# Wide products: the high-weight and the low-weight matmuls of a half, one phase after the other or tile by tile

## The reference, cut to what matters

```python
def conv_ffn(x, w_up, conv_w, conv_b, w_down):
    h = causal_dwconv(x @ w_up, conv_w, conv_b)
    gate, up = jnp.split(h, 2, axis=-1)
    return (jax.nn.gelu(gate) * up) @ w_down
```

## Time and profile before

| | |
|---|---|
| median of 3 runs | 3481.41 us (3480.82 to 3483.87) |
| span of the profiled execution | 3479.9 us |
| TensorE busy | 3388.8 us (97%) |
| VectorE, ScalarE busy | 2255.3 us (65%), 1729.5 us (50%) |
| DMA | 563.65 MB, mean 162 GB/s |
| mean granted TensorE clock | 0.992 |

### The profile page before, as it was taken

The page is one execution under the profiler, slowest core; times in us unless marked ns, Lnnn a source line. Parts: engine busy times, 40 slices in busy tenths (PEclk is TensorE's granted clock), DMA queues, the critical chain, the costliest instruction groups (busy, mean ns, idle before and its releaser), DMA issues.

```text
span 3479.9 us, 51413 instructions
## 1 busy us (share of the span) xinstructions
PE 3388.8 (97%) x20556; PEld 2996.1 (86%) x20556; DVE 2255.3 (65%) x2857; ACT 1729.5 (50%) x2142; POOL 0.2 (0%) x4
## 2 busy tenths in 40 slices
PE   9999998999999999999989999999999999999998
PEld 7888998888888888888878888888888888888887
DVE  6487676666666456555676666755666668556685
ACT  5473234565656335434366556643453555444553
POOL 0000000000000000000000000000000000000000
PEclk9999999999999999999999999999999999999999
DMA  7351034555554554432535544455454533544342
GB/s 278 147 189 47 2 122 146 193 186 183 185 193 151 193 183 179 176 134 77 195 145 193 187 180 187 160 188 184 174 192 147 194 121 146 194 149 188 126 165 102
DMA packets 45943, 563.65 MB, mean 162 GB/s; under 512 B 4928, under 2 KB 7120, under 8 KB 9168
## 3 DMA queue, kind: packets, MB, share of 16 engines
q1 hardware_dynamic: 45776, 561.27, 43.7%
HBM read 559.13 MB, written 2.12 MB: 161 GB/s over the span
## 4 chain that ended last, share of the span: by engine, by line
PE 88%; DVE 6%; ACT 3%; issue 2%; DMA 1%; SPq 0%; DVEq 0%; ACTq 0%
PE bank L765 38%; PE bank L769 20%; PE bank L860 8%; PE bank L865 4%; PE bank L894 3%; PE bank L878 2%; DVE ring L2250 1%; ACT spl_r L1609 1%; PE bank L789 1%; PE bank L1172 1%; DVE spl_r L2250 1%; DVE scr_r L2250 1%; PE bank L699 1%; PE bank L695 1%; PE bank L693 1%
## 5 line engine op out<-in xcount | busy, mean ns | idle before, releaser
L2250 DVE TENSOR_TENSOR spl_r<-ring,spl_r 128x2048 fp32r<-128x2048 f32 (+2 forms) x425 | 951.6, 2240 | 528.2 <-ACT spl_r L1609 526.4
L765 PE MATMUL bank<-all_r,spl_r 128*128 128x512 f32 x4960 | 1200.5, 394 | 5.4 <-ACT spl_r L1609 5.4
L1609 ACT ACTIVATE spl_r<-ring 128x2048 fp32r<-128x2048 f32 x409 | 781.9, 1912 | 612.9 <-PE bank L769 472.0
L765 PEld LDWEIGHTS bank<-all_r,spl_r 128*128 128x128 f32 x4960 | 915.2, 188 | 194.6 <-issue 7.9
L769 PEld LDWEIGHTS bank<-all_r,spl_r 128*128 128x128 f32 x5008 | 642.4, 191 | 28.9 <-DVE spl_r L2250 5.0
L769 PE MATMUL bank<-all_r,spl_r 128*128 128x256 f32 x5008 | 650.4, 283 | 3.7 <-DVE spl_r L2250 3.7
L860 PE MATMUL bank<-scr_r,dsp_r 128*128 128x512 f32 x1408 | 345.2, 393 | 11.6 <-ACT dsp_r L1609 6.1
L2250 DVE TENSOR_TENSOR dsp_r<-ring,dsp_r 128x1408 fp32r<-128x1408 f32 x128 | 208.0, 1625 | 222.5 <-ACT dsp_r L1609 222.5
L1609 ACT ACTIVATE dsp_r<-ring 128x1408 fp32r<-128x1408 f32 x128 | 176.6, 1380 | 281.2 <-PE bank L865 276.7
L860 PEld LDWEIGHTS bank<-scr_r,dsp_r 128*128 128x128 f32 x1408 | 256.4, 188 | 61.8 <-ACT scr_r L1619 6.8
L765 PE MATMUL bank<-scr_r,spl_r 128*128 128x512 f32 x1168 | 282.5, 394 | 3.4 <-ACT spl_r L1609 3.4
(11 more groups left out here) (403 smaller groups left out, 3002.8 us busy)
## 6 DMA issues: line engine op xcount, KB each, us to landing
ring<-in_up SPq DMA_DIRECT2D x88, 2048.0 KB, 7.9
ring<-in_down SPq DMA_DIRECT2D x64, 1408.0 KB, 6.0
ring<-in_ib SPq DMA_DIRECT2D x34, 2048.0 KB, 8.0
ring<-in_pg SPq DMA_DIRECT2D x16, 2048.0 KB, 8.2
ring<-in_out SPq DMA_DIRECT2D x16, 2048.0 KB, 7.9
ring<-in_in SPq DMA_DIRECT2D x12, 2048.0 KB, 8.1
ring<-in_ec SPq DMA_DIRECT2D x11, 2048.0 KB, 8.5
ring<-in_ea SPq DMA_DIRECT2D x8, 2048.0 KB, 10.9
```

The lines of the kernel that those rows point to most:

```text
L765: mm(b[:, :], WHI[half][:, kk, :], pair(name, kk), start=kk == 0, stop=False, skip_group_check=True)
L1609: A(high[half], w[:, :, half * P:(half + 1) * P], ACT.Copy).then_inc(S["w_hi"], count)
L2250: return V.tensor_tensor(out, a, b, op)
```

## The change

Within a half the two phases become one: for each tile the 512-column matmul with the high weights is followed at once by the 256-column matmul with the low weights. The wait for the low weights (`w_lo`) stands ahead of the first matmul of the half, where it stood between the phases. The same is done in the down product. In a `first` half the order of the matmuls stays as it was; only the form of the loop differs. `both_halves`, `first_piece` and the plain `product` are not touched, and neither are the lists of ScalarE, VectorE and the DMA queue.

```diff
@@ wide_half
                     from_low(0, early)
                     if early < DT:
                         from_high(early, DT)
-                else:
-                    for kk in range(DT):
+                pe.wait_ge(S["w_lo"], at(HALF0[name] + half + 1, k, i, 2))
+                for kk in range(DT):
+                    if not first:
                         mm(b[:, :], WHI[half][:, kk, :], pair(name, kk), start=kk == 0, stop=False,
                            skip_group_check=True)
-                pe.wait_ge(S["w_lo"], at(HALF0[name] + half + 1, k, i, 2))
-                for kk in range(DT):
                     one = mm(main, WLO[half][:, kk, :], rhi[:, kk, :], start=False, stop=kk == DT - 1,
                              skip_group_check=True)
@@ down
                             pe.wait_ge(S["w_hi"], ready)
+                            pe.wait_ge(S["w_lo"], ready)
                             for kk in range(FC):
                                 mm(b[:, :], DHI[half][:, kk, :], pair(name, piece * FC + kk),
                                    start=piece + kk == 0, stop=False, skip_group_check=True)
-
-                            pe.wait_ge(S["w_lo"], ready)
-                            for kk in range(FC):
                                 one = mm(main, DLO[half][:, kk, :], HHI[:, piece * FC + kk, :], start=False,
                                          stop=piece == 3 and kk == FC - 1, skip_group_check=True)
```

## The result

The changed kernel takes 3615.33 us in the median of three runs (3613.87, 3615.33 and 3617.10; a fourth, of 6201.66 at a granted clock of 0.782, is left out here and below, and with it the median would be 3616.22) against 3482.09 before: 1.0381 times the time, 95% interval 1.0367 to 1.0395. It is 133 us or 3.8% slower; forecast were 3570 us and 3515 to 3620.

What follows compares the result with a forecast made beforehand. TensorE was taken as the bound: number of matmuls times pitch, plus short waits. Added waits of 65 + 2 + 9 + 6 + 6 = 88 us, pitch 0, took the span from 3479.9 to 3568, so 3570 us; range 3515 to 3620.

Steps and rivals of the forecast that it cites:

- the chain through the in-order lists: Up products: splits, addition, scaled copy, convolution and gelu run in sequence before half 0's low weights, 12.02 us, 13.43 with table load.
- The up products (65 us): Up products, half 0 starts only when its low weights come: 11.95 us a piece, 0.76 more for each of 86, 65 us.
- the rival: Follow-up with ScalarE's list rearranged: low split late through busy VectorE or matmul order, under 20 us gained; no chance given.
- Idle time: Sign to look for: idle before wide matmuls grows from some 5 us to about 80, nearly all on up products' half 0.
- The down products (2 us): Down products: no wait in the steady part, late first halves cost 1 us for each layer, 2 us.
- The gate products (9 us): Gate products: a chain like the up product's costs 3 us plus 2.3 for the first piece in pg0; both together 9 us.
- The mixers and all others (12 us): Mixers: 6 us in the first one's input product where VectorE is late, 6 us for some ten halves before output products.
- Pitch (0): All changed products: alternating a wide and a narrow matmul keeps the pair at 0.348 us, so no change was taken.
- rival C: All changed products: the alternating order hurts, a pair takes 0.356 us, +48 us, 3618 us in all; chance 0.09.
- F, the faster side: All changed products: narrow loads hide under wide matmuls, pair about 0.315 us, -198 us less 88 of waits, 3370 us; chance 0.10.
- D: Waits are paid once as each product starts, 86 up pieces cost nothing: some 20 us, 3501 us; chance 0.05.
- E: Each half waits as long as its low weights are late now, 129 us in up products, 3640 us and over; chance 0.05.

## Why the prediction was right

The time lies in the range and the direction was right; the amount, 88 us, was too small: 133 by the medians, 133.7 by the spans. The mechanism that carries most of it, the chain through the in-order lists, was right. The pitch and the ends of the up products were not, and one of the prediction's own signs of being wrong came true: a half of a down product differs from 3.83 by over 0.03, for 44 of 61 in layer 0 and 33 of 61 in layer 1 take 3.88 to 3.89. Step by step:

- *The up products (65 us).* Right in place, mechanism and period of the steady part: 11.98 us for a piece with the wait alone, 11.95 forecast; cut in both lists, 67.7 us come back. In the changed kernel a piece takes 12.03 us in layer 0 and 12.07 in layer 1, a little over the 11.9 to 12.0 that were forecast, for there the order adds to it. The cut needed both lists: the first one alone was a test that nearly spoke for the rival, since a wait of the same size stood behind it.
- *The step that was mis-sized: "The change costs 0.76 us for each of 86 pieces: 65 us".* With the wait alone the two up products cost 83 us. The 76 pieces of their steady part cost 59.4, as forecast. The other ten, the first and the last four by this path of each product, cost 23.6 where the same price gives 7.6. There stand three waits of 2.7 to 3.9 us in each product, where the steady part has 0.9 and 1.2, and only behind these three does the lower clock stand in an up product. The rows name ScalarE's rounding copy for the waits of 2.7; no run takes it out of the list. The prediction read pieces of the steady part alone.
- *The clock, a term that the prediction doesn't have.* 17.0 of the 28.4 us more of busy time in that run are in matmuls at the lower clock. The other 10.2, at the waits, are no term of their own in a reckoning from start to start, as the prediction's is.
- *Idle time.* Ahead of the wide matmuls it was to grow from some 5 us to about 80; on the line with that 5.4 it became 86.9. "Nearly all on half 0 in the two up products" is right in part: in them it is all on half 0, but they have 69.3 of the 111.6 us on the three lines of wide matmuls.
- *The down products (2 us).* Mis-sized: 3.3 + 2.7 = 6.0. At their start in the changed kernel stands a wait of 3.94 us, where it was 1.61 before, and the clock is at 0.5 about a microsecond behind it. The steady part has no waits, as forecast.
- *The gate products (9 us).* 4.1 + 5.5 = 9.6. *The mixers and all others (12 us).* 19.1, of which 5.9 lie ahead of the first up product; which of them cost what was not taken apart.
- *Pitch (0).* Mis-sized, rival C in part: 21.8 us by the order alone; on top of the wait 15.9 by the spans (3613.6 - 3597.7) and 12.7 by the medians. That is about +0.003 for a pair, at the edge of the band that I gave the forecast (0.345 to 0.351) and a third of C's 0.008. That the blocks of four at the kernel's start have just this 0.351 is luck: blocks of four in the down products took 0.349. The two single pitches at a boundary (0.35 together) did not exclude it.
- *Together* the terms are short by 18 us (up products), 4 (down), 1 (gate), 7 (others) and, for the pitch, 16: 46 of the 133.7.
- *F, the faster side*, falls: no stream of narrow and wide matmuls came below 0.347 for a pair. With it falls, for these loads and this order, the reading of the Trainium skill's figures (TensorE: Matmul & The Clock Gate, "Back-to-back issue gap") as 325 ns; that section calls its N/2.4 + 2.5 the gap of an isolated matmul. D and E fall with the period of 11.98.

## What to carry to other kernels

A wait that moves ahead of work which covered it costs what the cover was worth: read from the timeline how long after the new place the signal comes, and follow back what makes it late, through the in-order lists of the other engines, to the event that starts it. If that event is the end of the waiting engine's own work, the delay feeds back and the period is that of the loop, neither the sum of the latenesses nor once. Do this for the first and the last pieces of a loop by themselves, where the lists hold other instructions: here ten pieces of 86 cost over a quarter of what the up products lose. To the waits add the time at the lower clock behind the longer ones, here 17 us beside 89 of idle time. And when a list is rearranged to cut such a chain, look in every engine's list for the instruction that was hidden behind the one moved.

## What the runs showed of the hardware

Alternating 512 and 256 columns has two steady pitches with the same instructions. In the timeline of the run with both lists rearranged ten halves (160 pairs) take 689.38 - 633.91 = 55.47 us, 0.347 for a pair; in the changed kernel one half (16 pairs) takes 774.75 - 769.11 = 5.64, 0.353. The steady up pieces of the run with both lists rearranged, which wait for nothing, have one value in each layer: 11.09 us (0.347 for a pair) in layer 0 and 11.31 (0.353) in layer 1; in phases, with the same lists, a piece takes 11.13 (0.348).

```profile
633.91 0.39 PE L766 MATMUL bank<-all_r,spl_r 128*128 128x512 f32 x1
...
689.38 0.39 PE L766 MATMUL bank<-all_r,spl_r 128*128 128x512 f32 x1
```

```profile
769.11 0.40 PE L766 MATMUL bank<-all_r,spl_r 128*128 128x512 f32 x1
...
774.75 0.40 PE L766 MATMUL bank<-all_r,spl_r 128*128 128x512 f32 x1
```

In the first the wide pitch is 230 ns and the narrow one 116 or 117, over and over. In the second they run in a cycle of three pairs, 232 + 118, 240 + 120, 236 + 114, and a wide matmul lasts 395 to 403 ns and not 391. A stream keeps its pitch over many halves, and it can change after a wait: in the changed kernel the halves that begin at 727.52 and at 750.86 have the short one, that of 763.38, after a wait of 1.19 us, the long one. The phases of before have a trace of the same: at 1018.84 the first 5 wide matmuls after the change from narrow to wide start 228 to 236 ns apart instead of 227, and about a microsecond later it is over; 64 of the 76 halves of layer 0's steady up product look alike. In the changed kernel's down products, halves of 11 pairs, the same shows as two lengths: 44 of 61 halves in layer 0 and 33 of 61 in layer 1 take 3.88 to 3.89 us, and 8 and 20 take 3.81 to 3.82, as 11 pairs of 0.353 and 0.347 make. The mean over a kernel depends on which of the two its streams fall into; what chooses was not found. The short one is below the 0.348 of the phases, so a kernel that always had it would gain, and none here does in all its products. The weight loads last 188 to 191 ns in the mean, before and after, longer than the 107 ns of the prediction's estimate.

The lower clock follows the longer waits, but not each of them. In the run with the wait alone it stands behind or around all waits of 2.69 to 4.10 us that the up, down and gate products have ahead of their wide matmuls, five in each layer; in the changed kernel two such waits, of 2.73 and 2.74 us (at 1101.22 and 2344.28), have none.
